# VectorE takes the retention's step ahead of the long convolution's taps, and the taps rest every second turn beside the retention's gate groups too

## What is computed

```python
h = rmsnorm(x, norm_mix_pre[l])
proj = h @ w_in[l]                       # q k v g_ret sc_b sc_c sc_x cf_a cf_b gate_logits
o = head_groupnorm(retention_chunkwise(rotary(q), rotary(k) / 8, v))     # 4 heads
y_ret = (silu(g_ret) * o) @ w_ret_out[l]
y_sc = (sc_b * causal_dwconv(sc_c * sc_x, sc_conv_w[l])) @ w_sc_out[l]   # 3 taps
c = causal_dwconv(cf_a * sigmoid(cf_b), cf_conv_w[l], cf_conv_b[l])      # 31 taps
y_cf = silu(layernorm(c, cf_ln_g[l], cf_ln_b[l])) @ w_cf_out[l]
merged = gate0 * y_ret + gate1 * y_sc + gate2 * y_cf
x = x + rmsnorm(merged @ w_o[l], norm_mix_post[l])
# then a gated feed-forward with a 3-tap convolution, and the second block
```

## Time and profile before

| what | value |
|---|---|
| three runs | 1870.03, 1867.89, 1865.99 us; median 1867.89 us |
| profiled execution | span 1870.4 us from first to last instruction; no other time of it is reported, it stands 2.5 us over the median and 0.4 us over the slowest of the three runs |
| TensorE matmul | 1811.5 us busy, 97% of the span |
| VectorE | 1364.4 us, 73% |
| ScalarE | 1076.2 us, 58% |
| GpSimd | 187.5 us, 10% |
| chain that ended last | TensorE 78%, VectorE 11%, ScalarE 5% |
| mean granted TensorE clock | 0.988 |

### The profile page before, as it was taken

How to read it: one execution, slowest core, us unless ns; L and a number is a source line. 1 busy time by engine, 2 the same in 40 slices (tenths; PEclk the granted TensorE clock), 3 DMA queues, 4 the chain that set the end, 5 groups by cost and what they waited for, 6 DMA issues and landing times.

```text
span 1870.4 us, 36335 instructions
## 1 busy us (share of the span) xinstructions
PE 1811.5 (97%) x14784; PEld 1768.1 (95%) x14784; DVE 1364.4 (73%) x2385; ACT 1076.2 (58%) x1812; POOL 187.5 (10%) x200
## 2 busy tenths in 40 slices
PE   8999999999999999999999999999998999999998
PEld 8899999999899999999889888999998998899998
DVE  6897789867889789866767767655558587676553
ACT  5455656655355666654676685545455757755542
POOL 1012410001003410001111003000002010030000
PEclk9999999999999999999999999999998999999999
DMA  7445536564545536554445644566554375355553
GB/s 283 168 152 187 185 124 203 193 206 155 187 148 180 181 128 200 189 196 135 155 137 167 196 136 129 181 197 193 194 160 140 126 200 160 128 170 180 194 195 108
DMA packets 90342, 320.08 MB, mean 171 GB/s; under 512 B 10528, under 2 KB 12992, under 8 KB 90048
## 3 DMA queue, kind: packets, MB, share of 16 engines
q1 hardware_dynamic: 90176, 317.75, 52.2%
HBM read 310.60 MB, written 1.08 MB: 167 GB/s over the span
## 4 chain that ended last, share of the span: by engine, by line
PE 78%; DVE 11%; ACT 5%; issue 3%; POOL 1%; DMA 1%; SPq 0%; DVEq 0%; ACTq 0%; POOLq 0%
PE big L582 71%; PE small L582 5%; DVE L L1097 3%; PE small L581 2%; DVE POOL L1454 2%; ACT H L1874 2%; DVE POOL L1324 1%; DMA POOL<-POOL 1%; POOL POOL L2470 1%; ACT POOL L2258 1%; DVE gates L1341 0%; DVE POOL L1286 0%; ACT POOL L2296 0%; POOL POOL L2449 0%; SPq L2613 0%
## 5 line engine op out<-in xcount | busy, mean ns | idle before, releaser
L582 PE MATMUL big<-HH,H 128*128 128x256 f32 x3344 | 950.1, 284 | 6.2 <-DVE gates L1341 3.5
L582 PE MATMUL big<-HL,H 128*128 128x256 f32 x3344 | 933.7, 279 | 3.8 <-DVE HL L1232 3.6
L582 PE MATMUL big<-HH,L 128*128 128x256 f32 x3344 | 932.6, 279 | 0.0
L1097 DVE TENSOR_TENSOR L<-F,H 128x1024 fp32r<-128x1024 f32 x574 | 702.4, 1232 | 196.4 <-ACT H L1874 195.0
L1874 ACT ACTIVATE H<-F 128x1024 fp32r<-128x1024 f32 x582 | 610.3, 1054 | 207.5 <-PE big L582 204.4
L582 PEld LDWEIGHTS big<-HH,H 128*128 128x128 f32 x3344 | 634.8, 190 | 11.2 <-DVE gates L1341 4.2
L582 PEld LDWEIGHTS big<-HL,H 128*128 128x128 f32 x3344 | 633.5, 189 | 7.8 <-DVE HL L1232 5.4
L582 PEld LDWEIGHTS big<-HH,L 128*128 128x128 f32 x3344 | 632.6, 189 | 0.0
L582 PE MATMUL big<-FH,H 128*128 128x256 f32 x848 | 240.1, 283 | 0.0
L582 PE MATMUL big<-FL,H 128*128 128x256 f32 x848 | 236.2, 278 | 0.0
L582 PE MATMUL big<-FH,L 128*128 128x256 f32 x848 | 236.1, 278 | 0.0
(11 more groups left out here) (238 smaller groups left out, 1805.7 us busy)
## 6 DMA issues: line engine op xcount, KB each, us to landing
F<-in_stream SPq DMA_DIRECT2D x582, 512.0 KB, 3.8
POOL<-POOL SPq DMA_DIRECT2D x32, 128.0 KB, 4.2
POOL<-head_rows SPq DMA_DIRECT2D x8, 256.0 KB, 5.0
X<-in_x SPq DMA_DIRECT2D x2, 512.0 KB, 4.4
POOL<-POOL SPq DMA_DIRECT2D x16, 64.0 KB, 3.2
out_x<-X SPq DMA_DIRECT2D x1, 1024.0 KB, 3.9
POOL<-in_decay SPq DMA_DIRECT2D x1, 768.0 KB, 10.9
POOL<-POOL SPq DMA_DIRECT2D x8, 96.0 KB, 5.1
```

The costliest lines, as they stand in the source:

```text
L582: return pe.e.matmul(out_, lhsT, rhs, start=start, stop=stop)
L1097: v.tensor_tensor(L[:, j % NR, :], F[:, j % NF, :], H[:, j % NR, :].bitcast(F32), ALU.subtract).then_inc(s_lo, 1)
```

## The change

`Steps` gets a method that puts a task at the head of the list. VectorE adds the retention by it, so that in each turn the retention's step comes before the taps. The order on the other engines stays. On all four engines the flag `slow` is raised for the g_ret groups too.

```diff
@@ class Steps
+    def add_first(self, name, task):
+        self.tasks.insert(0, (name, task))
@@ tensor_program, vector_program, scalar_program and pool_program, settle
-                    slow[0] = m.label[0:2] == "sc"
+                    slow[0] = m.label[0:2] == "sc" or m.label == "g_ret"
@@ vector_program, settle
                         elif name[:5] == "head_":
                             beside.add(name, head(m.l, name[5:]))
+                        elif name == "retention":
+                            beside.add_first(name, retention(m.l))
                         else:
                             beside.add(name, TASKS[name](m.l))
```

## The result

| | median us | lowest to highest | runs |
|---|---|---|---|
| kernel before | 1868.35 | 1855.49 to 1874.47 | 18 |
| changed kernel | 1876.24 | 1863.44 to 1887.79 | 18 |

The ratio is 1.0044, its 95% interval 1.0024 to 1.0063: the change makes the kernel slower by 4.5 to 11.8 us. The forecast was 1863.9 us and faster; the time lies above the whole range. The profiled execution of the changed kernel has a span of 1872.4 us at a mean clock of 0.989, against 1870.4 us and 0.988. Each run's time stands 1.7 to 1.9 us over the span of its core. So the execution with the span of 1870.4 us took some 4.3 us more than the median of its three runs, not 2.5 as I had it: an execution slower than usual.

What follows compares the result with a forecast made beforehand. TensorE, busy 97%, bounds the kernel, so gains come from its waits or clock: 10.7 us removed less 6.6 paid in two layers, say 4.0, gives 1863.9 us on the median; range 1857.5 to 1870.5.

Steps and rivals of the forecast that it cites:

- the decay product at head 0: TensorE's waits for L1414, 2.66 us in layer 0 and 3.82 in layer 1, were to vanish, with the low clock.
- The decay product of heads 1 and 3: Tap now behind L1419: TensorE waits 0.32 us, 0.44 with restart, at each head; 0.9 us a layer.
- before the reciprocal: In gate2 VectorE, with the reciprocal now first, waits for ScalarE's root: some 0.8 us idle.
- The adds' wait: TensorE's wait for GpSimd's adds behind the last tap grows from 0.67 to 2.2 us: 1.5 a layer, bounds 0 and 3.
- the spreading product's: TensorE reaches the long convolution's spreading product early and waits 0.9 us; with restart 1.0 a layer, 0 to 1.5.
- a sign of being wrong: Any low clock behind L2470, a wait for L1414 at head 0 above 0.5 us, or a tail without waits.
- What the change takes away: Decay product's waits at heads 0 and 2, slow clock and restarts over two layers: 10.7 us removable, between 9 and 10.7.
- The starved adds: GpSimd's three adds took 5.43 us beside VectorE's low parts; a hand-over would save some 2 us, but none was counted.
- The clock behind the adds: Clock loss at the adds' product, decided near 2.5 us of waiting; forecast wait 2.2 just under it; loss 1.7 us.
- the rival: *Slower*, 12%: last tap lags 3 us, TensorE waits 3.7 at the adds, clock costs 1.7 more; 1870.6 us.
- The y groups' banks: Behind the spreading product the tail's last four steps sit among short y groups, four banks covering: 0.1 us a layer.
- 1.5 + 1.0 + 0.1 - 0.2: Tail's price a layer: adds 1.5, spreading product 1.0, banks 0.1, less 0.2 us for two more groups at faster pace.

Runs made afterwards that it cites:

- the pair: Two unread small products, of 256 and 128 columns, put into feed-forward group fg4 of every layer; added to the kernel before: 1863.36 us, ratio 0.9963.
- run 5: The kernel before with two unread small products (256 and 128 columns) in fg4 of every layer, on one chip with run 6: 1864.58 us, ratio 0.9960.
- run 4: The kernel before with two unread small products (256 and 128 columns) in fg4 of every layer, first time: 1863.36 us, ratio 0.9963.
- run 6: The changed kernel with the two unread small products in fg4 of every layer: 1869.68 us, ratio 0.9974 to the kernel before.
- run 14: The changed kernel with the two unread small products in fg4, repeated on one chip with run 13: 1869.45 us, ratio 0.9984 to the kernel before.
- run 13: The kernel before with the two unread small products in fg4, repeated in a later set: 1864.46 us, ratio 0.9946 to the kernel before.
- Run 1: The changed kernel once more, unaltered, for a second trace: 1877.66 us, ratio 1.0046 to the kernel before.

## Why the prediction was wrong

**What was right.** The mechanism, at each place. No wait for the decay product at head 0, and a clock of 1.00 from 70 to 90 and from 500 to 520 us. The decay product of heads 1 and 3 is late, by 0.15 us where 0.32 was said. VectorE is idle 0.68 us before the reciprocal (0.8 said) and 0.62 before the first L1434 (0.7). The adds' wait is 2.14 us (2.2), the spreading product's 0.73 and 0.78 (0.9). A sum in it is off: for heads 1 and 3 it has TensorE wait 0.32 us, but its own times, 89.15 and 88.89, give 0.26. The clock did fall behind the adds, which I had named as a sign of being wrong. The forecast missed in three sizes, told below, and in the assumption of a fixed pace.

**The step "What the change takes away" is the first that failed.** It read 10.7 us from one execution, and that was an extreme one; 3.6 to 4.9 us were there to take. VectorE comes into the g_ret groups from the rotation, where it waits for transfers (L1286). Its timeline in the kernel before, layers 0 and 1, then in the kernel before with the pair (there L1293):

```profile
48.38 1.29 DVE L1286 TENSOR_TENSOR POOL<-POOL,CO 128x512 f32<-128x512 f32 x2 [3.72 <-DMA POOL<-POOL]
...
479.85 1.29 DVE L1286 TENSOR_TENSOR POOL<-POOL,CO 128x512 f32<-128x512 f32 x2 [5.08 <-DMA POOL<-POOL]
```

```profile
48.01 1.29 DVE L1293 TENSOR_TENSOR POOL<-POOL,CO 128x512 f32<-128x512 f32 x2 [3.09 <-DMA POOL<-POOL]
...
479.29 1.30 DVE L1293 TENSOR_TENSOR POOL<-POOL,CO 128x512 f32<-128x512 f32 x2 [1.97 <-DMA POOL<-POOL]
```

The longest such wait of a layer varies from 1.6 to 5.1 us over the traces of this study. Eight of them have the order and the rests of before. In these TensorE's wait at head 0 is 1.15 to 3.82 us where VectorE's wait for the transfers was over 3 us, and 0.74 to 1.21 us where that was under 2.6. TensorE's waits for the decay product were 6.8 us in all in the trace that I had, the longest 3.82, and 2.9 in that of run 5, the longest 2.18. Another trace of the same program (run 4) has 2.3 us in four waits, none over 1.2, and no low clock behind them. From the first column sum of each of the two layers to its last spreading product of the retention, the changed kernel with the pair (run 6) is 4.9 us shorter than run 5 in all, and 1.6 us shorter than run 4; run 14 is 3.6 us shorter than run 13. I had taken 10.7, less 1.8 for heads 1 and 3.

**The starved adds** went by the row, not by the hand-over that I had read out of the Trainium skill's rule (SBUF — State Buffer, Who interferes with whom); the rule speaks of one instruction, not of several in a row. GpSimd's timeline of the changed kernel:

```profile
167.86 5.39 POOL L2475 TENSOR_TENSOR POOL<-POOL 128x256 f32<-128x256 f32 x3 [29.42 <-DVE POOL L1457]
```

Beside VectorE's three low parts, back to back from 167.70 for 3.49 us, the three adds took 5.39 us again, the longest 3.91, as the 5.43 us of the earlier trace rows. A hand-over after each instruction would have made them shorter; this trace shows none.

**The clock behind the adds is the second.** It was in the rival, not in the sum: "The point from which it decides lies near 2.5 us of waiting: the same product ran its 0.70 us after 2.44, and 1.22 us after 2.53". Twelve waits of 2.13 to 2.15 us at the adds' product, in six traces, now stand against that: the clock fell behind eight of them, and behind 2.18 us at head 0 as well (granted 0.50 from 78 to 80 us in run 5). A fall costs about 1.5 us. Two rows were no ground for a threshold. Eight falls in twelve, at 1.5 us each, are about 1 us a layer that the sum left out. By the prediction's own numbers the lost clock alone would have left the gain at about nothing; what lies beyond that is the gain that was too large and the banks.

**The y groups' banks are the third.** "With four banks of cover; I count 0.1": measured 0.94 and 0.86 at the early y groups and 1.31 and 1.28 for 0.56 and 0.57 at the first y2 group in the changed kernel, 1.6 to 1.7 a layer. I did not test why: the four last steps of the long convolution stand in VectorE's turns of the y groups, and those turns are half as long as a gate turn.

**The sum with measured sizes.** A layer pays in the tail 4.7 us by the pair of traces of runs 5 and 6 (5.0 and 5.5 us by those of runs 13 and 14) where I had 1.5 + 1.0 + 0.1 - 0.2 = 2.4. Two layers pay 9.4 to 10.5, and 4.9 and 3.6 come back at the heads: 4.5 and 6.9 us slower, against 5.1 and 5.0 measured. The two gains at the heads are single traces, and by run 4 it is 1.6. The forecast's shape, a gain at the heads and a price in the tail, held; its gain was twice and more too large and its price half of what it is. The slower rival had named the adds' wait with the clock loss, and of its parts the clock loss came, the lag of 3 us did not.

**What stays open.** Without the pair the medians differ by 7.9 us, with it by 5.0. The interval of the first (4.5 to 11.8) holds both, and whether the change also shifts the odds of the slow pace was not settled. Nor is it shown why the two parts together cost 3.7 us more than the sum of both. Run 1 against the first trace shows that the slow stages of the changed kernel are not always the same ones.

## What to carry to other kernels

Before a wait is priced, see it in more than one execution: a wait that is fed by late transfers can be three times as long in one trace as in the next, and the largest looks the most worth removing. When work is taken out of a full engine's turns and put back later, read the last consumer behind it: here one turn more of slack for the adds was worth 7.8 us in the changed kernel, more than the 3.6 to 4.9 that the reordering gave at the heads. And where two executions of one kernel differ by more than the change is worth, look for a stage that runs at two paces, and steady it before comparing.

## What was new about the hardware

- At a granted clock of 1.00, 256-column matmuls with their weight loads start either 113 or 117.8 ns apart, and in these traces a feed-forward stage of some 1580 of them keeps one pace. A lone unread product of 256 columns in its group fg4 gave the slow pace in all four stages (1887.4 us), a product of 256 columns followed by one of 128 the fast one (1863 to 1865 us); the same pair at another place did nothing. Whether it is the widths or the number of products that decides was not tested.
- The same wait of TensorE can end with either clock. Behind the twelve waits of 2.13 to 2.15 us for the adds the granted clock fell to 0.50 in eight cases. The product of the earlier trace rows waited 2.43 or 2.44 us 22 times over all traces, and the clock fell behind 14 of them. The length of a wait alone does not tell it.
